# Turning the norm factor from rows that GpSimd prepares, and new tokens' values in one transpose, in a two-layer decoder step

## The reference

```python
def rms_norm(x, g):
    y = xf * lax.rsqrt(jnp.mean(xf * xf, axis=-1, keepdims=True) + NORM_EPS)
    return (y * g.astype(jnp.float32)).astype(x.dtype)
h = rms_norm(x, norm_g) @ w_in        # keys, queries, values, gates of all mixers
k_a = rope(...); v_a = ...            # mixer A: three dilations (1, 4, 16)
k_slc, v_slc, k_win, v_win = ...      # mixer C: selected blocks and a window
x = x + merge(mixer A, mixer B, mixer C) @ w_out
```

## Time and profile before

| | |
|---|---|
| median of 3 runs | 915.12 us |
| the profiled execution, its own time | 913.02 us |
| its span, first to last instruction | 911.4 us |
| granted TensorE clock, mean over the span | 0.998 |
| busy: PE, DVE, ACT, POOL | 98%, 71%, 50%, 21% of the span |

### The profile page before, as it was taken

How to read it: one execution, slowest core, us unless ns; L and a number is a source line. 1 busy time by engine, 2 the same in 40 slices (tenths; PEclk the granted TensorE clock), 3 DMA queues, 4 the chain that set the end, 5 groups by cost and what they waited for, 6 DMA issues and landing times.

```text
span 911.4 us, 21368 instructions
## 1 busy us (share of the span) xinstructions
PE 894.7 (98%) x7904; PEld 837.2 (92%) x7904; DVE 647.6 (71%) x1449; ACT 454.4 (50%) x900; POOL 194.3 (21%) x321
## 2 busy tenths in 40 slices
PE   7999999999999999999999999999999999999997
PEld 6999998888888799999999999898888978999996
DVE  6999776677667467656769996676766565775664
ACT  6444665465443544334553447664654444443352
POOL 1200000348658300000000000013574771000000
PEclk9999999999999999999999999999999999999999
DMA  9762995736979873333675587866569899345321
GB/s 331 300 227 97 427 355 207 303 142 183 315 236 289 268 326 147 139 140 125 257 255 193 204 320 265 305 269 246 189 181 301 248 273 347 149 155 206 149 94 52
DMA packets 66359, 209.96 MB, mean 230 GB/s; under 512 B 12192, under 2 KB 49776, under 8 KB 56272
## 3 DMA queue, kind: packets, MB, share of 16 engines
q1 hardware_dynamic: 57200, 187.67, 56.2%
q0 software_dynamic: 8912, 20.92, 7.1%
q10 hardware_dynamic: 144, 0.01, 0.0%
HBM read 202.58 MB, written 41.36 MB: 268 GB/s over the span
## 4 chain that ended last, share of the span: by engine, by line
PE 89%; SPq 4%; DMA 3%; issue 2%; ACT 1%; DVE 1%; DVEq 0%; ACTq 0%
PE bank L1056 65%; PE bank L1316 8%; PE bank L1069 4%; SPq L880 4%; DMA paged<-in_pool 2%; PE bank L1194 2%; PE bank L1186 1%; PE bank L1350 1%; PE bank L1223 1%; PE bank L1447 1%; PE bank L1236 1%; PE bank L1249 1%; DMA x<-in_x 1%; PE bank L1418 1%; PE bank L1295 0%
## 5 line engine op out<-in xcount | busy, mean ns | idle before, releaser
L1828 DVE TENSOR_TENSOR big_r<-big,paged_r 128x1024 fp32r<-128x1024 f32 (+1 forms) x160 | 194.6, 1221 | 72.5 <-ACT paged_r L1582 71.5
L1056 PE MATMUL bank<-xnT_high_r,paged_r 128*128 128x288 f32 x768 | 231.4, 301 | 0.0
L1056 PE MATMUL bank<-xnT_r,paged_r 128*128 128x288 f32 x704 | 207.7, 295 | 0.0
L1056 PE MATMUL bank<-xnT_high_r,big_r 128*128 128x288 f32 x704 | 207.2, 294 | 0.0
L1582 ACT ACTIVATE paged_r<-big 128x1024 fp32r<-128x1024 f32 (+1 forms) x160 | 166.7, 1049 | 4.8 <-DMA big<-in_w_feat 2.7
L1056 PE MATMUL bank<-short_r,big_r 128*128 128x288 f32 x568 | 167.5, 295 | 0.0
L1056 PEld LDWEIGHTS bank<-xnT_high_r,paged_r 128*128 128x128 f32 x768 | 144.0, 188 | 4.0 <-issue 2.0
L1056 PEld LDWEIGHTS bank<-xnT_high_r,big_r 128*128 128x128 f32 x704 | 132.5, 188 | 0.0
L1056 PEld LDWEIGHTS bank<-xnT_r,paged_r 128*128 128x128 f32 x704 | 132.3, 188 | 0.0
L1056 PE MATMUL bank<-short_r,paged_r 128*128 128x288 f32 x440 | 130.9, 298 | 1.1 <-DVE big_r L1828 0.9
L1056 PE MATMUL bank<-kvp_r,paged_r 128*128 128x288 f32 x440 | 130.4, 296 | 0.0
(11 more groups left out here) (353 smaller groups left out, 1804.7 us busy)
## 6 DMA issues: line engine op xcount, KB each, us to landing
big<-in_w_tok SPq DMA_DIRECT2D x13, 2048.0 KB, 9.0
big<-in_w_feat SPq DMA_DIRECT2D x12, 2048.0 KB, 8.5
big<-in_w_gate SPq DMA_DIRECT2D x10, 2048.0 KB, 8.6
out_kept_dil<-in_cache_dil SPq DMA_DIRECT2D x16, 1020.0 KB, 13.3
paged<-in_pool SPq DMA_DIRECT2D x218, 64.0 KB, 4.2
big<-in_w_up SPq DMA_DIRECT2D x12, 1024.0 KB, 8.7
paged<-in_pool POOLq DMA_DIRECT2D x166, 64.0 KB, 4.6
big<-in_kv_win SPq DMA_DIRECT2D x4, 2048.0 KB, 8.9
```

What stands on the lines that cost most here:

```text
L1056: last = mm(out, l, r, start=(c == 0 and i == 0), stop=(c == n - 1 and i == 2))
L1828: v.tensor_tensor(l_part[:, rest], full[:, rest], h_part[:, rest].bitcast(FP32), ALU.subtract)\
```

## The change

The step `rnt` moves to after tile 12 in both layers. POOL takes a share in it: it waits for the norm factor and writes five rows of 128 numbers on one partition (the new tokens' 32 factors four times over, and each class's 64 factors twice over), and PE then makes seven transposes of whole rows, two from the plain row and five from these. The new tokens' values of four kinds are written side by side by ACT (the window tile now takes two ACT instructions instead of one), so `vturn` 3 is a single transpose, whose first 96 rows are `v_stack` directly. `vstack` is gone, the store of new values becomes four stores. The third transpose of `vturn` 0 takes 128 columns instead of 32.

```diff
-NEW_STORES = 3
+NEW_STORES = 6
...
-        if i == (2 if layer else 5):
+        if i == 12:
             out.append(("rnt",))
...
-    blocks = {(1, 1): [("gates",)], (4, 1): [("vstack",)], (10, 0): [("ghid",)],
+    blocks = {(1, 1): [("gates",)], (10, 0): [("ghid",)],
...
+    rn_rows = tanh[0:1, :, :].rearrange("p i n -> p (i n)")[:, 0:5 * P]
...
+                elif k == "rnt":
+                    pool.wait_ge(*inverted.at(("root",)))
+                    fresh = rnB[0:1, SEQ:T].unsqueeze(1).to_broadcast([1, P // NS, NS])
+                    nc.gpsimd.tensor_copy(rn_rows[:, 0:P].rearrange("p (j t) -> p j t", t=NS), fresh)
+                    for c in range(STEP):
+                        one = by_class(rnB[0:1, 0:SEQ])[:, c, :].unsqueeze(1).to_broadcast([1, 2, CLASS])
+                        last = nc.gpsimd.tensor_copy(rn_rows[:, P * (c + 1):P * (c + 2)].rearrange("p (h m) -> p h m", h=2), one)
+                    last.then_inc(*by_row_ready.inc("all"))
...
-                    n_new += store(o["values_new"][layer], v_new)
+                    for i in range(len(A_TYPES)):
+                        n_new += store(o["values_new"][layer][:, P * i:P * (i + 1)], v_stack[NS * i:NS * (i + 1), :])
+                    n_new += store(o["values_new"][layer][:, VCOL["win"]:VW], v_new[:, VCOL["win"]:VW])
...
                     pe.wait_ge(*inverted.at(("root",)))
                     pe.wait_ge(const_in, 16 * len(CONSTS))
-                    ordered = by_class(rnB[0:1, 0:SEQ])
-                    wait(pe, TR.is_free(s))
-                    for c in range(STEP):
-                        for h in range(2):
-                            mm(tr(s)[CLASS * h:CLASS * (h + 1), 3 + c:4 + c], ordered[:, c, :], ident[0:1, 0:1],
-                               start=True, stop=True, skip_group_check=True)
-                    transposes(s, [(tr(s)[0:PARTS[tt], tt:tt + 1], rnB[0:1, TOK0[tt]:TOK0[tt] + PARTS[tt]])
-                                   for tt in range(3)])
+                    pe.wait_ge(*by_row_ready.at("all"))
+                    rows = [rnB[0:1, 0:P], rnB[0:1, P:SEQ]] + [rn_rows[:, P * i:P * (i + 1)] for i in range(STEP + 1)]
+                    transposes(s, [(tr(s)[:, i:i + 1], z) for i, z in enumerate(rows)])
...
-                        else:
-                            sources = [new_tokens(i) for i in range(4)]
-                        transposes(s, [(tr(s)[0:PARTS[j - 1], P * i:P * (i + 1)], z) for i, z in enumerate(sources)])
+                        sources = [v_fresh] if j == 3 else \
+                            [v_near[:, mine], v_far[:, P * c:P * (c + 1)], v_far[:, P * (c + 1):P * (c + 2)], v_win[:, mine]]
+                        transposes(s, [(tr(s)[:, P * i:P * (i + 1)], z) for i, z in enumerate(sources)])
...
+                        else:
+                            f(v_win, pj(s)[:, 0:SEQ], ACT.Copy)
+                        f(v_fresh[:, NS * t:NS * (t + 1)], pj(s)[:, SEQ:T], ACT.Copy).then_inc(*PJ.release(s))
...
-                            last = f(v_new[:, 0:512], tr(s)[0:NS, :], ACT.Identity, scale=rn[0:NS, 2:3])
+                            f(v_stack, tr(s)[0:3 * NS, 0:P], ACT.Identity, scale=rn[0:3 * NS, 2:3])
+                            last = f(v_new[:, VCOL["win"]:VCOL["win"] + P], tr(s)[3 * NS:P, 0:P], ACT.Identity,
+                                     scale=rn[3 * NS:P, 2:3])
...
-                elif k == "vstack":
-                    act.wait_ge(*TR.is_used(("vturn", 3)))
-                    for t in range(1, 3):
-                        last = f(v_stack[NS * t:NS * (t + 1), :], v_new[:, P * t:P * (t + 1)], ACT.Copy)
-                    last.then_inc(*v_stacked.inc("all"))
```

More of the change, by code:

```diff
@@ L464, in trunk_program @@
     raw_v = oT[2]
[L465 to L471, removed]
+    v_flat = raw_v[:, :, :].rearrange("p t n -> p (t n)")
+    v_near, v_far = v_flat[:, 0:SEQ], v_flat[:, SEQ:3 * SEQ]
+    v_fresh, v_win = v_flat[:, 3 * SEQ:3 * SEQ + 4 * NS], v_flat[:, 3 * SEQ + 4 * NS:4 * T]
+    near_blocks = v_near.rearrange("p (c m) -> p c m", c=STEP)
+    far_blocks = v_far.rearrange("p (c t m) -> p t c m", c=STEP, t=2)
     qTA = long[:, 0:3 * REP * SEQ].rearrange("p (t r n) -> p t r n", t=3, r=REP)
@@ L764, in trunk_program @@
     first_in = [nc.alloc_semaphore(f"first_weights{q}_in") for q in range(4)]
+    by_row_ready = sig("norm_factor_by_row", ["all"])
     g_in, const_in, late_in = [nc.alloc_semaphore(n) for n in ("norm_g_in", "constants_in", "late_constants_in")]
-    v_stacked = Signal(nc, "new_values_stacked", [(z, "all") for z in LAYERS])
     FIRST = gate_keys[0]
@@ L1149, in _ @@
                     if j == 0:
-                        transposes(s, [(tr(s)[0:PARTS[tt], P * tt:P * (tt + 1)],
-                                        prod[:, TOK0[tt]:TOK0[tt] + PARTS[tt]]) for tt in range(3)])
-                    else:
[L1153 to L1156, removed]
-                        else:
-                            sources = [new_tokens(i) for i in range(4)]
-                        transposes(s, [(tr(s)[0:PARTS[j - 1], P * i:P * (i + 1)], z) for i, z in enumerate(sources)])
+                        transposes(s, [(tr(s)[:, P * tt:P * (tt + 1)], prod[:, t0:t0 + P])
+                                       for tt, t0 in enumerate((0, P, T - P))])
+                    else:
+                        mine, c = slice(P * (j - 1), P * j), 2 * (j - 1)
+                        sources = [v_fresh] if j == 3 else \
+                            [v_near[:, mine], v_far[:, P * c:P * (c + 1)], v_far[:, P * (c + 1):P * (c + 2)], v_win[:, mine]]
+                        transposes(s, [(tr(s)[:, P * i:P * (i + 1)], z) for i, z in enumerate(sources)])
                 elif k == "feat":
@@ L1421, in _ @@
                     elif what == "anew":
-                        pe.wait_ge(*v_stacked.at("all"))
+                        pe.wait_ge(*TR.is_used(("vturn", 3)))
                         last = mm(out[:, 0:P], pt[0:3 * NS, 0:P], v_stack, start=False, stop=True, skip_group_check=True)
@@ L1511, in _ @@
                     act.wait_ge(*TR.is_full(s))
-                    f(rn[:, 0:2], tr(s)[:, 0:2], ACT.Copy)
+                    f(rn, tr(s)[:, 0:3], ACT.Copy)
                     f(rn_class, tr(s)[:, 3:3 + STEP], ACT.Copy)
@@ L1515, in _ @@
                         rows = slice(CLASS * h, CLASS * (h + 1))
-                        f(rn_tile[rows, :], tr(s)[rows, 3 + h:3 + STEP:2], ACT.Copy)
-                    f(rn[0:NS, 2:3], tr(s)[0:NS, 2:3], ACT.Copy).then_inc(*TR.release(s))
+                        last = f(rn_tile[rows, :], tr(s)[rows, 3 + h:3 + STEP:2], ACT.Copy)
+                    last.then_inc(*TR.release(s))
                 elif k == "nround":
@@ L1527, in _ @@
                     dst = raw_q[TILES[i][1]][:, TILES[i][2], :] if kind == "q" else raw_k[i // K_SLC][:, i % K_SLC, :] \
-                        if kind == "k" else prod[:, :] if i == V_SLC else raw_v[:, i - V_FIRST, :]
-                    if kind == "v" and TILES[i][1] in A_TYPES:
+                        if kind == "k" else prod[:, :]
+                    if kind == "v" and i != V_SLC:
                         t = i - V_FIRST
-                        classes = far_blocks[:, t - 1, :, :] if t else v_near[:, 0:SEQ].rearrange("p (c m) -> p c m", c=STEP)
-                        f(classes, by_class(pj(s)[:, 0:SEQ]), ACT.Copy)
-                        f(new_tokens(t), pj(s)[:, SEQ:T], ACT.Copy).then_inc(*PJ.release(s))
+                        if TILES[i][1] in A_TYPES:
+                            f(far_blocks[:, t - 1, :, :] if t else near_blocks, by_class(pj(s)[:, 0:SEQ]), ACT.Copy)
+                        else:
+                            f(v_win, pj(s)[:, 0:SEQ], ACT.Copy)
+                        f(v_fresh[:, NS * t:NS * (t + 1)], pj(s)[:, SEQ:T], ACT.Copy).then_inc(*PJ.release(s))
                         continue
@@ L1540, in _ @@
                         slc = slice(VCOL["slc"], VCOL["slc"] + P)
-                        for tt, n in enumerate(PARTS):
-                            last = f(v_prompt[:, tt, slc] if tt < 2 else v_new[:, slc], tr(s)[0:n, P * tt:P * (tt + 1)],
-                                     ACT.Identity, scale=rn[0:n, tt:tt + 1])
+                        for tt in range(3):
+                            rows = slice(P - NS, P) if tt == 2 else slice(0, P)
+                            last = f(v_prompt[:, tt, slc] if tt < 2 else v_new[:, slc], tr(s)[rows, P * tt:P * (tt + 1)],
+                                     ACT.Identity, scale=rn[rows, tt:tt + 1])
                         last.then_inc(*TR.release(s))
```

## The result

The changed kernel takes **923.15 us** (median of 6 runs, 918.91 to 924.37), the kernel before 915.72 (median of 6 beside it). The ratio is 1.0077 (95% interval 1.0064 to 1.009): slower by 0.8%. The forecast was 922.8, in a range of 918.8 to 928.5.

The account below looks back on a forecast made before the run. PE, busy 98% of the span, was taken as the bound. Layer 0's lateness 7.1 us, plus clock 1.7, less layer 1's 1.1, gave +7.7 us on the median 915.12: 922.8 us, 80% range 918.8 to 928.5.

Parts of the forecast that it names:

- The new wait: Layer 0, `rnt` after tile 12: PE waits for POOL's copies, queued behind page-number loads and stores; PE 7.4 us late.
- The price of a copy: POOL's five row copies before `rnt`: 0.6 us each, 3.0 us for five.
- an end of the range: Upper end for POOL's five copies: 5 us if DVE's two-input work holds them up too.
- Signal and transposes: Layer 0, after POOL's copies: 0.07 us for the signal to PE, 0.46 for seven transposes, 0.11 for the slower first step.
- The clock: Layer 0, after PE's wait: matmuls run at the lower clock for a while, costing 1.7 us (ends 0.5 and 2.5).
- Layer 1: PE gains 0.78 + 0.33 = 1.1 us there; POOL's copies finish 2.8 us before PE needs them.
- `vturn` 3: Each layer: the step loses three of its four transposes, saving PE 0.33 us.
- The reconfiguration: Rival, chance 0.15: POOL must be reconfigured before its first copy while PE waits, 3.8 us more, 926.6 us.
- Cheap copies with the clock kept: Rival, chance 0.15: copies of 0.1 us and a clock loss of 0.5 us, 3.7 us less, 919.1 us.
- POOL is in time: Rival, chance 0.08: POOL reaches `rnt` before 52.7 in layer 0, PE's saving remains: 914.0 us, or 912.9 if DVE gives way.
- the 1.48: Microseconds the old `rnt` costs PE after tile 5 in layer 0; only 0.3 counted as gained if POOL is in time.
- A step of 16 bytes in the source: Four of POOL's five copies read so; by a rule 0.4 us longer together, an estimate not in the sum.

Follow-up runs that it names:

- second experiment: Changed kernel with POOL loading its page numbers after its copies of layer 0 instead of ahead of all steps: 914.87 us, ratio 0.9996 to the kernel before.
- third: Changed kernel with `rnt` after tile 18 instead of tile 12 in layer 0, layer 1 unchanged: 915.25 us, ratio 0.9995 to the kernel before.
- the doubled copies: Changed kernel with POOL's five copies made twice in both layers, first into a spare row of another partition: 924.86 us, ratio 1.0107 to the kernel before.
- ACT's rows: Changed kernel with ACT writing the five rows after tile 5 (layer 1: 2), `rnt` after tile 6 (3): 914.53 us, ratio 0.9992 to the kernel before.
- second profile: Profile from running the changed kernel again with no edit: 922.57 us, ratio 1.0082 to the kernel before.

## Why the prediction was right

**The new wait** was named by its place, its partner and its cause. Without the page numbers ahead of it (second experiment), or with PE later (third), the slowdown is gone: this is shown by two edits that have nothing in common but the order of POOL against PE.

**The price of a copy**, taken as 0.6 of a possible 0.1 to 1.0: five took 2.75 us in the first profile and 2.94 in the second, against 3.0. The sum was right and its reason only partly, so that it came out so close is in part luck. I took it from the elements per partition; the doubled copies show 0.36 for a class copy with DVE silent, and 0.6 beside its two-input instructions. Nearly half of the price was DVE's doing, which had been named as an end of the range.

**Signal and transposes**: 0.07 + 0.46 = 0.53 us expected from POOL's end to the end of the seven, and 0.11 for the slower first step. In the first profile the copies end at 58.38 and tile 13 starts at 59.02: 0.64. In the second it is 0.95 (59.57 to 60.52), because there the transposes too ran at the lower clock. The 0.07 for the signal was an estimate that no row showed.

**The clock**: 1.7 us expected, 1.6 in the first trace and 1.4 in the second (60.52 to 63.56, 12 steps of tile 13). It fell to the same level after 2.9 us of standing still as after 6.1 us.

**Layer 1**, -1.1: no wait for POOL, `rnt` at 0.71 instead of 1.48. In the first profile tile 13 there is 2.25 us less late than the `vturn` of layer 0, of which the first two can hold 1.1 (0.33 in layer 0's `vturn` 3, 0.77 here); the other 1.1 lies at waits for cache pages in layer 0: before they are 1.1 and 1.0 us there, after only one of 1.1 is left. The sum had no term for this. That a later PE finds the pages landed is not shown: with `rnt` after tile 18 PE is only 1.3 us late after the `vturn` steps and makes up 2.1 us at the same place, and with ACT's rows it is 1.6 us late and makes up 0.1. These waits differ from one execution to the next.

**`vturn` 3**, -0.33 each. The timeline of PE in the changed kernel:

```profile
111.70 0.33 PE L1078 MATMUL bank<-ident,oT_c 128*128 128x128 f32 x1
111.86 0.49 PE L1078 MATMUL bank<-ident,prod 128*128 128x128 f32 x3
```

The transpose of the new tokens stands 0.16 ahead of the three of `vturn` 0; in the trace of before the first of the four starts at 103.85 and the three of `vturn` 0 at 104.30, 0.45 later. That is a saving of 0.29, a little under what was said, and the three of `vturn` 0 last 0.49 as before.

**The rivals.** The reconfiguration did not come: POOL's first copy starts at 55.63, with the store before it ending at 55.64. Cheap copies with the clock kept fell on both counts (2.75 us, clock at 0.50). That POOL is in time was false for this kernel, but its working is what holds once it is made true: it gave 914.0, a fall of 0.12%, with 0.3 of the 1.48 left after DVE's bank. The two kernels with the wait removed have 0.9996 and 0.9995, and DVE's bank takes 0.44 and 1.4 us. The working named the wrong tile: it had tile 8 wait for the second raw tile, and it is tile 7 that waits, for the first. What would be gained if that bank were freed sooner was not tried.

**The spread.** The step that read least well is the one that had no part in the sum: how far one profile stands for the median. PE's arrival and the end of POOL's loads each move by a microsecond or more between executions, so the wait was 2.9 in one profile and 6.1 in the next. The forecast took its sum from one trace and added it to the median. Followed through the second profile, which has POOL where the forecast had it, this works for layer 0: after the `vturn` steps PE is 8.9 us late (113.42 against 104.54), where 7.1 + 1.7 = 8.8 was forecast. From there to the end it makes up 2.3 us instead of 1.1, and the span is 6.6 us longer, not 7.7. The medians differ by 7.4.

So the last microsecond of the hit is luck. The two kept profiles of the changed kernel are each the shortest of their six (918.91 and 919.70), 4.2 and 2.9 us under their medians, where the one of before is 2.7 under its own, and no trace of a median execution was kept. One place that moves is seen: between 653.30 and 790.94 of the trace of before, seven of the other traces lose 0.8 to 3.0 us against it, at waits for cache pages and for what is made from them, while the changed kernel's two lose 0.3 and nothing.

## What to carry to other kernels

Before a step is given to an engine that looks idle (POOL had 22% busy time), read its queue in program order up to that step, with register loads, which busy time does not count, and with what they wait for: here 16.6 us of loads stood in front, and they could not begin before a transfer had landed at 36.4. Put the producer's end and the consumer's arrival on one time axis; if the first is later, either move the consumer behind six more tiles or move the queue's other work behind the producer. A saving on the busiest engine at a place where another engine's bank comes next is only worth the slack to that bank.

## What the hardware showed unexpectedly

**POOL and DVE hold each other up, instruction by instruction.** The first copy has the same shape everywhere, 128 numbers on one partition, yet lasts 0.28 us in layer 0 and 1.06 in layer 1 of the changed kernel. The timeline of DVE there, first in layer 1, then in layer 0:

```profile
496.72 2.36 DVE L1829 TENSOR_TENSOR big_r<-big,paged_r 128x1024 fp32r<-128x1024 f32 x2
...
55.47 0.80 DVE L1757 STREAM_SHUFFLE PT<-oT_a 128x576 f32<-128x576 f32 x1
56.30 0.94 DVE L1758 TENSOR_TENSOR PT<-PT,kvp 128x576 f32<-128x576 f32 x1
57.16 0.96 DVE L1759 TENSOR_TENSOR oT_a<-oT_a,kvp 128x576 f32<-128x576 f32 x1
```

In layer 1 the copy begins at 498.16, beside a two-input subtraction of 128x1024 which ends at 499.08, and the next copy starts at 499.18: it seems to have waited for that instruction's end. With the page numbers moved it is the same, 1.05 us with DVE's pair of the same line beside it. In layer 0 it stands beside a shuffle, with one input, and takes 0.28. The way back is seen too: the two-input instructions beside the class copies take 0.94 and 0.96 us, where the same lines take 0.76 and 0.75 with no copy beside them:

```profile
49.82 0.76 DVE L1758 TENSOR_TENSOR PT<-PT,kvp 128x576 f32<-128x576 f32 x1
50.50 0.75 DVE L1759 TENSOR_TENSOR oT_a<-oT_a,kvp 128x576 f32<-128x576 f32 x1
```

The Trainium skill, SBUF — State Buffer, section on the two separate sides of SBUF, says that the pair shared by the two engines is an exclusive lock: whichever starts first has it for the whole instruction. It says so for a VectorE instruction with two SBUF inputs against a GpSimd one that reads SBUF. These rows agree with it in the wait of the first copy and in the two-input condition.

**A step of 16 bytes in the source** cost little or nothing that can be told apart. With DVE silent a class copy takes 0.36 us; the copy without such a step takes 0.24 beside the shuffle (55.63 to 55.87) and 0.38 in the doubled copies (59.57 to 59.95), partly beside DVE. The rule of the GPSIMD Engine Reference of the Trainium skill, weighed in the prediction as 0.4 us for four, would be 0.1 each, an estimate; by the first pair of numbers it could be there, by the second not. It stays open.

**The clock at the start**, read from the distances of matmuls, rose at 9.65 us in one execution and at 18.09 in another. The work is the same, but in the later one PE also stood still for 0.57 us before 10.76 and for 0.56 us before 13.60. PE was 3.2 us late by this at tile 4 (25.65 against 22.46), and 2.5 us after tile 12. In this kernel that vanished in the wait; in a kernel without a wait it would be part of the spread.
